# Two layers of a hybrid model on one core: key halves, maxima, the dense head and the MLP's opening in another order

## What is computed

```python
for l in range(DEPTH):
    (..., nsa_q, nsa_kc, nsa_vc, nsa_ks, nsa_vs, nsa_kw, nsa_vw, nsa_gate) = split_columns(h @ w_in[l])
    y_a = mamba2_ssd(...)
    y_b = mla(...)            # 4 heads, causal softmax attention, 1024 keys
    y_c = retention(...)
    y_d = nsa(...)            # 4 heads; compressed, selected and window keys
    mix = jnp.concatenate([y_a, y_b, y_c, y_d], axis=-1) @ w_out[l]
    h = layer_norm(DEEPNORM_ALPHA * h + mix, ln1_g[l], ln1_b[l])
    ff = jnp.square(jax.nn.relu(h @ w_mlp1[l])) @ w_mlp2[l]
    h = layer_norm(DEEPNORM_ALPHA * h + ff, ln2_g[l], ln2_b[l])
```

## Time and profile before

| | |
|---|---|
| median of three runs | 2865.5 us (2863.94 to 2869.27) |
| the profiled execution, its own time | 2868.43 us |
| its span in the trace | 2866.6 us |
| mean granted clock of PE | 0.974 of 2.4 GHz |
| PE busy | 2732.7 us, 95% |
| DVE, ACT, POOL busy | 1797.8, 1136.9, 249.7 us |

### The profile page before, as it was taken

The page is one execution under the profiler, slowest core; times in us unless marked ns, Lnnn a source line. Parts: engine busy times, 40 slices in busy tenths (PEclk is TensorE's granted clock), DMA queues, the critical chain, the costliest instruction groups (busy, mean ns, idle before and its releaser), DMA issues. The chain is left out here.

```text
span 2866.6 us, 37139 instructions
## 1 busy us (share of the span) xinstructions
PE 2732.7 (95%) x13986; PEld 2187.6 (76%) x13986; DVE 1797.8 (63%) x2939; ACT 1136.9 (40%) x1817; POOL 249.7 (9%) x220
## 2 busy tenths in 40 slices
PE   5999989999989999999999999899999899999997
PEld 5899856655867887888889998566568688878886
DVE  5654454454787776786855544625547877758778
ACT  3422223434355554433433222234343555543343
POOL 3221212000000000000012212210000000000000
PEclk9999988999999999999999999889999999999999
DMA  4223233102315445986621233421032254579865
GB/s 168 65 67 102 89 100 73 32 1 81 96 65 174 144 146 197 385 307 241 220 85 59 63 94 96 105 46 30 1 110 89 90 160 144 155 249 369 288 229 189
DMA packets 254360, 387.29 MB, mean 135 GB/s; under 512 B 38608, under 2 KB 126800, under 8 KB 254184
## 3 DMA queue, kind: packets, MB, share of 16 engines
q1 hardware_dynamic: 254184, 384.92, 41.3%
HBM read 288.05 MB, written 96.83 MB: 134 GB/s over the span
## 5 line engine op out<-in xcount | busy, mean ns | idle before, releaser
L2734 ACT ACTIVATE att_PT<-att_ST 128x512 f32<-128x512 f32 (+2 forms) x244 | 135.1, 555 | 337.6 <-PE att_ST L2627 203.2
L1616 PE MATMUL mix_acc<-mix_whi,x_hi 128*128 128x256 f32 (+1 forms) x640 | 185.4, 290 | 0.0
L994 PE MATMUL dense_tr<-mlp_w,mlp_a 128*128 128x512 f32 x448 | 175.3, 391 | 5.6 <-DVE mlp_w L1292 5.6
L1618 PE MATMUL mix_acc<-mix_whi,x_lo 128*128 128x256 f32 (+1 forms) x640 | 180.0, 281 | 0.0
L1617 PE MATMUL mix_acc<-mix_wlo,x_hi 128*128 128x256 f32 (+1 forms) x640 | 179.9, 281 | 0.0
L996 PE MATMUL dense_tr<-mlp_w,mlp_a 128*128 128x512 f32 x448 | 174.4, 389 | 0.0
L995 PE MATMUL dense_tr<-mlp_w,mlp_a 128*128 128x512 f32 x448 | 174.3, 389 | 0.0
L994 PE MATMUL dense_acc<-mlp_w,mlp_a 128*128 128x512 f32 x448 | 174.3, 389 | 0.0
L996 PE MATMUL dense_acc<-mlp_w,mlp_a 128*128 128x512 f32 x448 | 174.3, 389 | 0.0
L995 PE MATMUL dense_acc<-mlp_w,mlp_a 128*128 128x512 f32 x448 | 174.3, 389 | 0.0
L644 POOL TENSOR_TENSOR norm_rstd<-norm_var,norm_power 128x1 f32<-128x1 f32 x32 | 29.8, 931 | 1476.7 <-DVE norm_var L624 1476.7
(11 more groups left out here) (432 smaller groups left out, 7488.9 us busy)
## 6 DMA issues: line engine op xcount, KB each, us to landing
mlp_w_raw<-w_mlp SPq DMA_DIRECT2D x124, 512.0 KB, 5.7
blocks<-h SPq DMA_DIRECT2D x32, 1792.0 KB, 8.2
mlp_a_raw<-blocks SPq DMA_DIRECT2D x72, 512.0 KB, 4.5
mlp_raw<-w_mlp SPq DMA_DIRECT2D x66, 512.0 KB, 6.0
ahead<-w_in SPq DMA_DIRECT2D x20, 1024.0 KB, 6.5
mlp_temp<-blocks SPq DMA_DIRECT2D x38, 512.0 KB, 4.7
residual<-h SPq DMA_DIRECT2D x32, 512.0 KB, 3.8
h<-residual SPq DMA_DIRECT2D x32, 512.0 KB, 9.2
```

What stands on the lines that cost most here:

```text
L994: pe.matmul(out, ah, wh, start=(ch == 0 and k == 0), stop=False, skip_group_check=True)
L1616: pe.matmul(out, xh, whi[b][:, k, 0:n], start=(k == 0), stop=False)
L1618: mm = pe.matmul(out, xl, whi[b][:, k, 0:n], start=False, stop=(k == KT - 1))
L2734: act.activation(PT[0:width, n % 3, c0:512], ST[0:width, n % 2, c0:512], ACT.Exp).then_inc(s.exp_ready, 1)
```

## The change

There are four parts, each in both layers.

- Attention, keys: `key_highs` starts at `KEYS0 = FIRST_HALF - 5`, so the four halves stand in steps 11 to 14. The first of the two instructions on `u` moves from step 14 to step 11.
- Attention, maxima of units 0 to 3: PE's turn of a unit follows the scores of the next unit, DVE's placing of a unit follows the maxima of the unit after the next.
- Dense head: ACT and DVE split the first block of `w_out` ahead of token tile 0, the second ahead of tile 1. PE does blocks 0 and 1 of tile 0 first, then those of tile 1; from block 2 on it goes as before.
- MLP opening: on ACT the copy of group 2's product 2 stands ahead of group 1's two activations; on DVE group 1's gather, rests and two quarters move behind group 2's first sums of weights (`rests`), and `block_sums(0)` stays.

```diff
--- before.py
+++ after.py
@@ -719,15 +719,21 @@
 
             turn_y(0)
             turn_y(1)
-            pe.wait_ge(s.y_lo, 4)
-            for k in range(KT):
+            for t in range(2):
+                pe.wait_ge(s.y_lo, 2 * t + 2)
+                for k in range(2):
+                    pe.wait_ge(s.wo_lo, k + 1)
+                    for half in range(2):
+                        products(t, half, k)
+            turn_y(2)
+            for k in range(2, KT):
                 pe.wait_ge(s.wo_lo, k + 1)
                 for t in range(2):
                     for half in range(2):
                         mm = products(t, half, k)
                         if k == KT - 1:
                             mm.then_inc(s.out_ready, 1)
-                if 1 <= k < NT - 1:
+                if k < NT - 1:
                     turn_y(k + 1)
             for t in range(2, NT):
                 pe.wait_ge(s.y_lo, 2 * t + 2)
@@ -745,15 +751,14 @@
                     act.activation(hi[:, 4 * half:4 * half + 4, here(t)],
                                    tr[:, 2 * (t % 2) + half, :].rearrange("p (k n) -> p k n", k=4), ACT.Copy).then_inc(s.y_hi, 1)
 
-            y_highs(0)
             for k in range(KT):
                 if k < 2:
                     act.wait_ge(ahead.sem, rows_loaded)
                 else:
                     act.wait_ge(wo_loaded[k % 4], 16 * ((k + 2) // 4))
                 act.activation(wo_hi[:, k, :], raw_of(k), ACT.Copy).then_inc(s.wo_hi, 1)
-                if k == 0:
-                    y_highs(1)
+                if k < 2:
+                    y_highs(k)
                 if k >= 3:
                     y_highs(k - 1)
             y_highs(NT - 1)
@@ -791,12 +796,11 @@
                 stats(dve, t, 1)
                 moments(dve, t)
 
-            y_lows(0)
             for k in range(KT):
                 dve.wait_ge(s.wo_hi, k + 1)
                 dve.tensor_tensor(wo_lo[:, k, :], raw_of(k), wo_hi[:, k, :].bitcast(F32), ALU.subtract).then_inc(s.wo_lo, 1)
-                if k == 0:
-                    y_lows(1)
+                if k < 2:
+                    y_lows(k)
                 if k >= 3:
                     y_lows(k - 1)
             y_lows(NT - 1)
@@ -1139,6 +1143,9 @@
                             activate(g, i)
                         elif i == 2:
                             if g == 2:
+
+                                activate(1, 4)
+                                activate(1, 3)
                                 square(1, 6)
                             square(g - 1, 7)
                     elif (g, i) == (0, 1):
@@ -1146,8 +1153,6 @@
                         activate(0, 3)
                     elif (g, i) == (1, 7):
                         square(0, 7)
-                        activate(1, 4)
-                        activate(1, 3)
                     if i == 7 and g != 1:
                         square(g, 6)
                     if p + RING < N:
@@ -1236,6 +1241,12 @@
                         mm = dve.tensor_tensor(stage[g % 2][:, i - 1, :], part[a], part[b], op)
                     mm.then_inc(s.blocks_ready, 1)
 
+                def rests(g):
+                    gather(g)
+                    rest12(g)
+                    rest21(g)
+                    rest1(g)
+
                 def collect(p):
                     g, i = order[p]
                     if g >= 2:
@@ -1248,18 +1259,17 @@
                             rest1(g)
                         elif i == 5:
                             block_sums(g - 1)
-                    elif (g, i) in ((0, 1), (1, 7)):
-                        if g:
-                            block_sums(0)
-                        gather(g)
-                        rest12(g)
-                        rest21(g)
-                        rest1(g)
-                        if g:
-                            quarter22(g)
+                        elif (g, i) == (2, 2):
+                            rests(1)
+                            quarter22(1)
+                            quarter11(1)
+                    elif (g, i) == (0, 1):
+                        rests(0)
+                    elif (g, i) == (1, 7):
+                        block_sums(0)
                     if i == 6 and g != 1:
                         quarter22(g)
-                    elif i == 7:
+                    elif i == 7 and g != 1:
                         quarter11(g)
 
                 def sum_of(item):
@@ -2433,6 +2443,8 @@
         compress_at = [CMP0 + j * (CMP1 - CMP0) // CMP_LEN for j in range(CMP_LEN)]
         MAX0 = CMP1 + 5
 
+        KEYS0 = FIRST_HALF - 5
+
         split_at = [FIRST_HALF + 6 + 2 * i if i < 4 else N0 + 2 + 2 * (i - 4) for i in range(NT)]
 
         first_units = [u for u in range(UN) if first_step[u] == 0]
@@ -2683,8 +2695,9 @@
 
                     for u_ in first_units:
                         maxima([(u_, at) for at in range(len(pieces[u_]))])
-                    for u_ in first_units:
-                        turn_maxima(u_)
+                        if u_:
+                            turn_maxima(u_ - 1)
+                    turn_maxima(first_units[-1])
                     for n in range(len(steps)):
                         for u_ in turned_before[n]:
                             turn_maxima(u_)
@@ -2734,8 +2747,8 @@
                         act.activation(PT[0:width, n % 3, c0:512], ST[0:width, n % 2, c0:512], ACT.Exp).then_inc(s.exp_ready, 1)
                         if n - 1 in ends:
                             copy_sum(ends[n - 1], n - 1)
-                        if FIRST_HALF <= n < FIRST_HALF + 4:
-                            key_highs(1 + (n - FIRST_HALF) // 2, (n - FIRST_HALF) % 2)
+                        if KEYS0 <= n < KEYS0 + 4:
+                            key_highs(1 + (n - KEYS0) // 2, (n - KEYS0) % 2)
                         if n == FIRST_HALF + 5:
                             act.wait_ge(s.t_loaded, 16)
                             act.activation(gates[:].rearrange("p t h b -> p t (h b)"), raw_t[:, :, 2 * HD:TOKV], ACT.Tanh, scale=0.5).then_inc(s.gate_tanh, 1)
@@ -2810,7 +2823,9 @@
                     dve.wait_ge(s.parts_set, 2)
                     for u_ in first_units:
                         maxima([(u_, at) for at in range(len(pieces[u_]))])
-                    for u_ in first_units:
+                        if u_ >= 2:
+                            place(u_ - 2)
+                    for u_ in first_units[-2:]:
                         place(u_)
                     for n in range(len(steps)):
                         for u_ in turned_before[n]:
@@ -2820,13 +2835,13 @@
                             dve.tensor_copy(peT[:], back[:, 0:CMP_LEN]).then_inc(s.pe_copied, 1)
                         if n - 2 in ends:
                             write(ends[n - 2])
-                        if n == CMP0 - 1:
+                        if n in (CMP0 - 4, CMP0 - 1):
+                            g0 = (CMP0 - 4, CMP0 - 1).index(n)
                             dve.wait_ge(s.kv_loaded, 16)
                             dve.wait_ge(s.pe_copied, 1)
-                            for g0 in range(2):
-                                dve.tensor_tensor(u[:, g0, :, :], kvT[:].rearrange("p (n j) -> p n j", j=CMP_STRIDE),
-                                                  peT[:, g0 * CMP_STRIDE:(g0 + 1) * CMP_STRIDE].unsqueeze(1).to_broadcast([P, NG, CMP_STRIDE]),
-                                                  ALU.add).then_inc(s.placed, 1)
+                            dve.tensor_tensor(u[:, g0, :, :], kvT[:].rearrange("p (n j) -> p n j", j=CMP_STRIDE),
+                                              peT[:, g0 * CMP_STRIDE:(g0 + 1) * CMP_STRIDE].unsqueeze(1).to_broadcast([P, NG, CMP_STRIDE]),
+                                              ALU.add).then_inc(s.placed, 1)
                         if n == FIRST_HALF + 4:
                             dve.wait_ge(s.t_loaded, 16)
                             dve.wait_ge(s.ones_set, 3)
```

## The result

The changed kernel takes 2844.6 us (median of four runs, 2841.42 to 2847.2) against 2865.6. The ratio is 0.9924, with a 95% interval of 0.9907 to 0.9942: 21.8 us less by the ratio, between 16.6 and 26.6 (the two medians lie 21.0 apart). The forecast was 2846, from a sum of 22.8 us. The profiled run took 2847.2 us, its span is 2845.4 us and its mean granted clock 0.977; before they were 2866.6 and 0.974.

What follows compares the result with a forecast made beforehand. PE was busy for 95% of the span, so only its waits and half-speed work could give time: 5.85 + 11.1 + 0.8 - 1.4 + 4.35 + 2.1 + 0 = 22.8 us off the profiled 2868.4, forecast 2846 us, range 2837 to 2857.

Steps and rivals of the forecast that it cites:

- Keys and the stall: Attention: sooner key halves let the queries land before ACT asks, removing PE's waits for an exponential, 5.85 us.
- the clock term: Attention: the half clock behind the stall goes with it, 2.2 us in layer 0 and 8.9 in layer 1, together 11.1.
- `u`: Attention: moving the first half to step 11 removes PE's wait of 1.6 us; half taken, 0.8 us gained.
- Maxima: Attention's opening: the new order of turns and placings loses 0.7 to 0.8 us per layer, 1.4 us in all.
- Dense head: Head's opening: PE's first products start sooner, 1.6 us in layer 0 and 2.75 in layer 1, 4.35 us of idle time.
- 2.1 us of clock: Dense head: half-speed work behind the idle time goes, half of it in layer 0 and all in layer 1.
- 1.8 us of idle time: Dense head, layer 0: idle time of PE expected to remain ahead of the first product; none in layer 1.
- MLP opening: MLP: the sooner copy of product 2 only moves PE's idle time by one product, term 0.
- the shift of the wait: MLP opening: PE's idle time moves to ahead of the product that needs `copy5`, some 7 us.
- The reason given for the end: MLP opening: the next weights' transfer, landing at 865.82 after DVE waited 5.07 us, ends it, and none of this moves.
- The bound of 14.8 us: MLP opening: rival that it gains after all, 14.8 us, time 2830.8 us, chance 6%.
- the long half-clock stretch: Attention, layer 1: this stretch may be what the profiled run, 2.9 us over the median, has over the others.

Runs made afterwards that it cites:

- experiment 11: Changed kernel with ACT's copy of group 2's product 5 right behind that of product 2, product 1's copy in its old place: ratio 0.9898, median 2837.4 us.
- experiment 9: The changed kernel timed once more beside the kernel before, on one chip: ratio 0.9921, medians 2842.7 and 2864.2 us.
- Experiment 10: Changed kernel with SP loading group 3's weights ahead of the store of group 0's blocks, no copy moved: ratio 0.9921.
- experiment 1: Kernel before with only the four key halves on ACT moved to steps 11 to 14: ratio 0.9983, 4.9 us less.
- experiment 2: Kernel before with the key halves at steps 11 to 14 and `u` in two pieces at steps 11 and 14: ratio 0.9955, 12.9 us less.

## Why the forecast was right, and which of its steps were not

**Keys and the stall.** Each step came as written: the transfer at 469.26 (469.2 was worked out; POOL began 0.6 us sooner than assumed, at 461.20, and its two pairs took 8.0 us and not 7.4), the stall gone, full clock behind it, 11.66 us between the landmarks (11.9 in layer 0 by the sum). The size of the clock term was off. 11.1 us came from one execution whose layer 1 had a stretch of 20 us at half clock. Ten stretches with the stall took 7.46 us more than sixteen without it; twice that is 14.9 us, against 16.95 in the sum (5.85 + 11.1). By the timed runs keys and `u` together gave 12.9. Without the 5.85 us of idle time the table leaves 9.1 us for the clock, where the sum had 11.1.

**`u`.** I priced it by itself, at 0.8 us. Alone it gave nothing that could be told; behind the keys it gave the difference between 4.9 and 12.9 us, as far as two comparisons with intervals of some 4 us to either side can say. What the sum missed is that the key halves bring POOL's work into the time of `u`. I had followed POOL's pair from the keys to the queries' load, but had not asked what lies beside it on DVE.

**Maxima.** A loss of 1.4 us was forecast. The opening is 0.51 us longer in layer 0 of the changed profile and 1.46 in layer 1, 0.37 in the mean, and the steps behind it are 1.36 us shorter in the mean, which the sum did not have. The likely value is near nothing; one timing of two has it at 4 us more, which stays open.

**Dense head.** 4.35 us of idle time were forecast, and the first product comes 4.3 us sooner; 2.1 us of clock and 2.1 found. One sign was wrong: 1.8 us of idle time were to be left in layer 0, and the changed profile has none. There the transposes ran at the lower clock and took the time themselves (3.65 us instead of 1.94). Where they run at full clock (experiment 11, layer 1: 1.94 us), PE waits 1.61 us behind them, and the first product comes 3.55 us behind their start all the same. In the changed kernel's own profile the clock term is small (99.19 and 98.90 against 99.29 and 99.69); only the other profiles show its mean. The prediction weighed a rule of the Trainium skill against this ("TensorE: Matmul & The Clock Gate", Part 4: PE-mode transpose), by which transposes don't count for the clock and the 2.1 us would not come. They came. More directly: in the profile of experiment 9 PE does the 16 transposes behind 2.32 us of idle time at the lower level, and the first product follows at 690.81:

```profile
687.26 3.29 PE L710 MATMUL dense_tr<-ident,h 128*128 128x128 f32 x16 [2.32 <-PEq L131]
...
690.81 0.50 PE L716 MATMUL dense_acc<-out_whi,x_hi 128*128 128x512 f32 x1 [0.26 <-DVE x_lo L784]
```

The clock in the stretches from the transposes' beginning on:

```profile
686.50:689.50 3.00, 2.24 (x11) 2.27 (x12) 1.17 (x2) 1.92 (x3) 0.10 (x1) 0.52 0.44 101
...
689.50:690.00 0.50, 0.50 (x4) 0.50 (x3) 0.50 (x2) 0.50 (x2) 0.00 (x0) 0.50 0.98 401
...
690.00:690.50 0.50, 0.50 (x5) 0.31 (x3) 0.50 (x2) 0.50 (x1) 0.00 (x0) 0.95 1.03 418
```

It is 0.95 from 690.0 to 690.5, so 2.4 GHz came back ahead of the product, and PE had done nothing but transposes since the idle time. For these transposes (`pe.transpose` in the code, in float32) the rule does not hold; for other types no run here shows it.

**MLP opening.** The number 0 was right, and so was the shift of the wait (some 7 us ahead of the product that needs `copy5`; it is 6.74). The time between the block sums did not shrink either. The reason given for the end was wrong. I wrote that the weights' transfer ends the opening, since DVE stood waiting for it. Experiment 10 takes that wait away, and nothing changes. In the changed kernel PE ran through after `copy5` in layer 0 and came to product 7 at 866.37, the old 874.32 less 7.95, because the 6.74 us of idle time and the first matmuls at the lower clock behind it (starts 0.43 us apart instead of 0.23) fill up what the sooner copy of product 2 had given. The transfer is the second bound, right behind (in layer 1 of that profile PE did wait, 1.28 us, for the copy of product 1): it shows as soon as the copies are sooner (experiment 11), and taking both away gives 17.4 us. The bound of 14.8 us that the prediction kept for a gain here was about the size of what lay in this opening, but this part of the change doesn't reach it.

**The sum.** That 22.8 us stood so near the 21.8 measured is in part luck. The sum was taken off the profiled execution, 2.9 us above the median. In that execution the stretches of the table's first row took 228.58 and 235.22 us, together 2.7 more than twice the mean of ten; so the long half-clock stretch was what it had over the others, as the prediction suspected, and from the median the same sum is 19.9 us. The clock term that was too large and the 0.8 us for `u` then stand against a loss on the maxima that the table doesn't have.

## What to carry to other kernels

Move all the copies that free a bank ahead of the work that waits for something else, not one of them: a single one only hands the wait to the next product. Where an engine waits for a transfer, ask whether PE would have run on without that wait, before the transfer is called the bound; two bounds that lie close are seen only when both are taken away. When a step is moved, look at what now runs beside it on the other engines (here POOL beside DVE), and measure the parts together as well as alone. A stall's price is idle time plus the clock behind it, and the second is to be read from several executions.

## What the runs showed of the hardware

- DVE's additions of `u` (128 x 1024, two inputs from SBUF) take 2.36 us for two with POOL at rest, 4.29 beside POOL's subtractions and copy on the keys (experiment 1); a single one takes 1.21 with POOL at rest and 1.65 beside the end of a subtraction and a copy (experiment 2). The Trainium skill ("GPSIMD Engine Reference", section 8, Key points) says that GpSimd shares its SBUF interfaces with VectorE and contends with instructions of two SBUF inputs; the trace agrees.
- The same list of instructions, with a stall of 2.7 to 3.0 us in it, took 227.7 to 235.3 us in ten stretches. Without the stall sixteen stretches lay within 0.13 us of one another.
- What costs most to tell apart here is the scatter of the executions: the kernel before ran between 2854 and 2880 us, and the two small parts could not be priced within it: their timings alone and within the whole contradict each other.
